# Gate and value projections of two transformer layers: seven block products in place of eight

## The chip, the cores and the metric

The kernel runs on one core of a Trainium2 chip. The metric is the device time of one execution in microseconds (us), lower is better; the number that counts is the median over runs. All data are float32.

The core has a matrix engine (TensorE, "PE" in the profile; its weight loads are the row "PEld"), a vector engine (VectorE, "DVE"), an activation engine (ScalarE, "ACT"), GpSimd ("POOL") and SyncE ("SP"), which here only issue DMAs. They run in parallel and meet through semaphores. TensorE writes to eight PSUM banks of 128 x 512 float32.

## The reference

The first block has two layers over 256 tokens of width 1024. Each layer is

```
ada = silu(c) @ w_ada[l] + b_ada[l]            # six sections: sh1, sc1, g1, sh2, sc2, g2
u = h * (1 + sc1) + sh1
y = mixer(u, w_in, ...)                        # mLSTM + dilated attention, then
                                               # (sig(g_a)*(a @ w_a) + sig(g_b)*(b @ w_b)) @ w_out
h = layer_norm(ALPHA * h + g1 * y) * ln1_g + ln1_b
u = h * (1 + sc2) + sh2
y = (silu(u @ w1) * (u @ w3)) @ w2             # w1, w3: 1024 x 2816; w2: 2816 x 1024
h = layer_norm(ALPHA * h + g2 * y) * ln2_g + ln2_b
```

The second block (256 latent and 256 context tokens) is a windowed attention with an MLP ("attn"), then a gated linear attention with an MLP ("gla"; 256 tokens only). It takes its modulation `ada` from its own matrix for two conditions.

## The kernel before

**Panels.** All weights come from HBM in half panels of 4 k-tiles x 512 columns (1 MB), through a ring of `RING` = 7 slots in SBUF. SyncE (L2951) loads half panel n once half panel n-7 has been released; TensorE releases a panel by an increment that rides on one of its next matmuls (`release`, L528).

**PE's order** is written out by hand in `@block.tensor` (L482). `feature_tiles` (L541) computes two feature tiles (128 features each) for all 256 tokens: 16 matmuls of 128 x 128 weights on 256 moving columns. One such call is one PSUM bank. The profile shows two records for each float32 matmul: 32 for such a call.

**PSUM banks** are handed out by `open_tile` (L485): a new tile takes the next of the eight banks in turn, and TensorE first waits until the tile that held this bank eight openings ago is drained:

```
b = st["next"]
...
if b in st["tenant"]:
    drained(*st["tenant"][b])
```

**End of the mixer (L817 to L828).** The products with `w_a` and `w_b` ("WA 0" to "WA 3", "WB 0" to "WB 3", two feature tiles each) are mixed on VectorE into `MIX` (L2410 to L2427). TensorE waits for "mix 3" and then runs the output projection "WO" (four tiles of 8 matmuls on 512 columns). VectorE adds the residual and normalises token tile 0, then token tile 1 (L2429 to L2433).

**Gate and value projections (L828 to L846).** TensorE transposes token tile 0 (`tile_transposes("U", 0)`), and ScalarE modulates it into `UT`. `half_tiles` (L572) then computes W1 0 and W3 0 for token tile 0 alone; it waits for the first half of the modulated features ahead of k = 0 and for the second ahead of k = 4. Token tile 1 is transposed and modulated (first half by ScalarE, second by VectorE, L2434), the second half of W1 0 and W3 0 follows, and then `feature_tiles` for W1 j, W3 j, j = 1 to 10. ScalarE takes silu of each W1 tile; VectorE multiplies with W3 (L2437 to L2442). A product of a W1 and a W3 panel has 8 blocks: k halves (2) x feature halves (2) x token halves (2).

**VectorE beside that (L2436 to L2454).** `affine("U")` (L1998): four operations of 128 x 1024 on the residual. Then the modulation turns: `ada_turn` (L2294) multiplies one 1 MB piece of `w_ada` (two operations of 128 x 1028 for one condition, four for two) and frees its slot; GpSimd (L2962) loads the next piece into one of two slots. Layer 0 takes 12 such turns here, layer 1 takes 20, of which 16 have two conditions. Engines work in order: whatever stands behind a waiting operation waits too.

**Winograd's form of Strassen's product** is in the kernel already, for W2 (L857 to L889, with `down_sums`) and for the MLPs of the second block (`fast_mlp`, L965, L2612): seven block products in place of eight, with sums of weight quarters (`panel_sums`, L2546), sums of token blocks (`token_sums`, L2565) and sums of the products (`first_sum`, L2582, and `product_sums`, L2589) on VectorE. `ORDER` is (1, 2, 4, 5, 7, 6, 3). The first panel goes by `FIRST_ORDER` (1, 2, 5, 7, 6, 3, 4): products 1 and 2 need token tile 0 alone. In the MLP of gla, a block product is 8 matmuls on 128 moving columns: the shape that the change uses.

Of the kernel before, what the change touches and what calls it, by code (L numbers as in the profile page):

```python
# [23 lines left out]
P = 128  # L24
# [223 lines left out]
def program(nc, a, out, marks):  # L248
    with ExitStack() as ctx:
# [183 lines left out]
        def combos(stage, nh):  # L433
# [5 lines left out]
                    for l in range(2) for w in ("w_mlp_in", "w_mlp_out", "w2")}  # L439
# [9 lines left out]
        down_out = area(M2["UT2"], KD, 2 * T)  # L449

# [31 lines left out]
        def _(pe):  # L482
# [151 lines left out]
            for l in range(DEPTH):  # L634
# [203 lines left out]
                j = 2  # L838
                for p in range(1, 6):
                    w1, w3 = panel(), None  # L840
                    for n in range(2 if p < 5 else 1):
                        feature_tiles(f"W1 {j}", w1, n, UT)
                        w3 = w3 or panel()
                        feature_tiles(f"W3 {j}", w3, n, UT)
                        j += 1
                    release(w1 + w3)  # L846
# [486 lines left out]
        def _(act):  # L1333
# [86 lines left out]
            for l in range(DEPTH):  # L1420
# [136 lines left out]
                act.wait_ge(dve_done, DV.at("h U"))  # L1557
                layer_params(l + 1)

                act.wait_ge(dve_done, DV.at("ln1 1"))  # L1560
                act.dma_start(ctx_early, a["ctx"].rearrange("(t p) n -> p t n", p=P)).then_inc(params_in, 16)
                if l == DEPTH - 1:
                    act.dma_start(area(M["CST"] + 2 * P, NC2), a["consts_attn"]).then_inc(par2_in, 16)
                for j in range(FFT // 2):
                    if j >= 4:
                        act.wait_ge(dve_done, DV.at(f"W3 {j - 4} drained"))
                    act.wait_ge(pe_done, PE.at(f"W1 {j} full"))
                    drain(f"W1 {j}", sg[:, j % 4, :], ACT.Silu).then_inc(act_done, AC.drained(f"W1 {j}"))
# [372 lines left out]
        def _(dve):  # L1941
# [143 lines left out]

            def down_sums(p, kg, i):
# [213 lines left out]
            for l in range(DEPTH):  # L2300
# [87 lines left out]
                for u in range(SLOTS // 2):  # L2388
# [14 lines left out]
                    for n in (2 * u, 2 * u + 1):  # L2403
                        dve.wait_ge(act_done, AC.at(f"slot exp {n}"))
                        V.reciprocal(att[:, n % 2, 3, :], att[:, n % 2, 2, :]).then_inc(dve_done, DV.step())
                        dve.wait_ge(dve_done, DV.count)
                        for tt in range(NT):
                            ts(SC[n % 2][:, tt, :], SC[n % 2][:, tt, :], att[:, n % 2, 3, tt:tt + 1], None, ALU.mult).then_inc(
                                dve_done, DV.step(f"probs {n}" if tt else None))
                for p in range(2):  # L2410
                    for n in range(2):
# [5 lines left out]
                            dve_done, DV.drained(f"WA {j}"))  # L2417
                    for n in range(2):
# [16 lines left out]
                dve.wait_ge(rows2_in, 16 * (l + 1))  # L2435
                affine("U")  # L2436
                for j in range(FFT // 2):  # L2437
                    dve.wait_ge(pe_done, PE.at(f"W3 {j} full"))
                    ps = tile(f"W3 {j}")
                    dve.wait_ge(act_done, AC.at(f"W1 {j} drained"))  # L2440
                    tt_(GT[:, 2 * j:2 * j + 2, :].rearrange("p a b -> p (a b)"), ps[:, :], sg[:, j % 4, :], ALU.mult).then_inc(
                        dve_done, DV.drained(f"W3 {j}"))  # L2442
                    if j < 2:
                        for q in turns[2 * j:2 * j + 2]:
                            ada_turn(q, [("ada", 0)])
                        if j == 1:
                            gate("g2")
                    elif j < 6:
                        for q in range(2 * j - 4, 2 * j - 2):
                            ada_turn(q, [("next", 0)] if l + 1 < DEPTH else [("next", 1), ("nextx", 2)])  # L2450
                    elif j < 10 and l == DEPTH - 1:
                        for q in range(2 * j - 4, 2 * j - 2):
                            ada_turn(q, [("ada", 1), ("adax", 2)])
                    if j == 8:  # L2454
                        down_token_sums(0, 0)
                down_sums(0, 0, 5)
# [88 lines left out]

            def panel_sums(name, n, i, after):  # L2546

                a11, a12, a21, a22 = quarters(n)
                if i == 5:
                    for m in (n, n + 1):  # L2550
                        dve.wait_ge(panel_in[m % RING], 16 * (m // RING + 1))
                    if after:
                        dve.wait_ge(pe_done, PE.at(f"{after} full"))
# [490 lines left out]
```

## Time and profile before

| | us |
|---|---|
| median of 3 runs | 2424.16 (2416.7 to 2425.68) |
| profiled execution | 2416.46, its span 2414.7 |
| TensorE busy | 2324.4 (96%) |
| VectorE busy | 1253.5 (52%) |
| ScalarE busy | 494.2 (20%) |
| gate and value stage, layer 0 (446 to 600) | TensorE 154.00 of 154, VectorE 47.22, DMA share 0.65 |
| gate and value stage, layer 1 (1097 to 1252) | TensorE 153.86 of 155, VectorE 108.43, DMA share 0.79 |
| mean granted TensorE clock | 0.992 of full |

A timeline row tells: start and duration in us, engine, line, operation, output <- input with shapes, count, and in brackets the idle time of that engine ahead of it with what ended it. Rows that stand close are merged ("x56"). "PEclk" is the granted clock, 1.00 for 2.4 GHz and 0.50 for 1.2 GHz.

### The profile page before, as it was taken

How to read it: one execution, taken by the hardware profiler on the slowest of the kernel's cores; microseconds unless marked ns; L12 is line 12 of the kernel's file. 1: busy time of each engine (PE TensorE's matmuls, PEld its weight loads, DVE VectorE, ACT ScalarE, POOL GpSimd, SP SyncE). 2: the span in 40 equal slices, each digit the busy share in tenths (PEclk: the TensorE clock that was granted, in tenths of full speed). 3: DMA queues.
4: the chain of work that ended last, by engine and by line, in shares of the span. 5: the costliest groups of instructions: out<-in, count | busy, mean ns of one | idle time of the engine just before them, and what ended most of it. 6: DMA issues, size and time to landing. Idle time of an engine off the chain costs nothing.

```text
span 2414.7 us, 27153 instructions
## 1 busy us (share of the span) xinstructions
PE 2324.4 (96%) x10982; PEld 1835.2 (76%) x10982; DVE 1253.5 (52%) x2360; ACT 494.2 (20%) x1048; POOL 62.6 (3%) x93
## 2 busy tenths in 40 slices
PE   7999999999999999999999999999999999888998
PEld 5888587788768876868887655588888874567987
DVE  5764311432746432125777266775566455556666
ACT  1222320100011223101011355312200032432200
POOL 0100000000000000000000000000000000000000
PEclk9999999999999999999999999999999999999999
DMA  9853433674475333336874101433333245134442
GB/s 392 321 210 106 156 122 126 233 289 166 175 283 196 134 110 145 124 136 249 305 288 166 35 36 36 148 113 134 121 123 140 79 141 187 74 113 170 161 158 79
DMA packets 163499, 391.18 MB, mean 162 GB/s; under 512 B 6448, under 2 KB 10928, under 8 KB 160560
## 3 DMA queue, kind: packets, MB, share of 16 engines
q1 hardware_dynamic: 136736, 285.03, 32.7%
q0 software_dynamic: 24080, 93.69, 10.6%
q10 hardware_dynamic: 2560, 10.72, 1.2%
q8 instruction: 88, 1.44, 0.2%
q14 instruction: 35, 0.29, 0.0%
HBM read 388.37 MB, written 1.05 MB: 161 GB/s over the span
## 4 chain that ended last, share of the span: by engine, by line
PE 91%; DVE 4%; ACT 2%; DMA 1%; issue 1%; DVEq 0%; SPq 0%; ACTq 0%
PE bank L503 89%; DVE arena L1946 2%; PE bank L501 2%; ACT arena L1335 2%; DVE arena L1952 1%; DMA arena<-in_w_ada 1%; ACT arena L1338 1%; DVE arena L1949 0%; DMA arena<-in_x 0%; DVE arena L2827 0%; ACT L1335 0%; DVE arena L2084 0%; DVE arena L2011 0%; DVE arena L2015 0%; DVE arena L2859 0%
## 5 line engine op out<-in xcount | busy, mean ns | idle before, releaser
L503 PE MATMUL bank<-arena 128*128 128x256 f32 (+6 forms) x10494 | 2267.1, 384 | 47.4 <-ACT arena L1335 15.2
L503 PEld LDWEIGHTS bank<-arena 128*128 128x128 f32 (+2 forms) x10494 | 1777.0, 189 | 524.7 <-issue 283.7
L1946 DVE TENSOR_TENSOR arena<-arena 128x1024 f32<-128x1024 f32 (+9 forms) x497 | 374.8, 767 | 231.0 <-PE bank L503 194.3
L1952 DVE SCALAR_TENSOR_TENSOR arena<-arena 128x1028 f32<-128x1028 f32 (+6 forms) x367 | 304.5, 845 | 101.6 <-DMA arena<-in_w_ada 66.7
L1335 ACT ACTIVATE arena<-arena 128x512 f32<-128x512 f32 (+5 forms) x386 | 196.7, 533 | 709.8 <-DVE arena L1946 357.5
L1946 DVE TENSOR_TENSOR arena<-bank,arena 128x512 f32<-128x512 f32 (+3 forms) x123 | 83.7, 690 | 471.4 <-PE bank L503 445.0
L1338 ACT ACTIVATE arena<-bank 128x512 f32<-128x512 f32 (+1 forms) x227 | 127.4, 596 | 707.8 <-PE bank L503 667.2
L1335 ACT ACTIVATE arena<-bank 128x256 f32<-128x256 f32 (+2 forms) x99 | 41.3, 438 | 400.3 <-PE bank L503 399.6
L1946 DVE TENSOR_TENSOR arena<-arena,bank 128x256 f32<-128x256 f32 (+2 forms) x172 | 85.4, 521 | 64.6 <-PE bank L503 59.8
L2970 POOL DMA_DIRECT2D arena<-in_w_ada x88 | 61.8, 702 | 2141.4 <-DVEq L1961 2135.4
L1952 DVE SCALAR_TENSOR_TENSOR arena<-bank,arena 128x254 f32<-128x254 f32 (+2 forms) x184 | 78.0, 468 | 51.4 <-PE bank L501 35.2
L501 PE MATMUL bank<-arena 128*128 128x128 f32 x488 | 65.9, 286 | 33.3 <-DVE arena L1949 17.6
L501 PEld LDWEIGHTS bank<-arena 128*128 128x128 f32 x488 | 58.8, 147 | 44.7 <-issue 21.3
L1949 DVE TENSOR_SCALAR arena<-arena 128x512 f32<-128x512 f32 (+8 forms) x278 | 80.3, 322 | 20.5 <-ACT arena L1335 12.7
L1952 DVE SCALAR_TENSOR_TENSOR junk<-arena 128x1028 bf16<-128x1028 f32 x64 | 78.6, 1229 | 6.3 <-DVE arena L1952 2.3
L1952 DVE SCALAR_TENSOR_TENSOR arena<-arena,bank 128x512 f32<-128x512 f32 (+1 forms) x40 | 24.8, 645 | 101.3 <-PE bank L503 97.1
L1949 DVE TENSOR_SCALAR arena<-bank,arena 128x256 f32<-128x256 f32 (+1 forms) x112 | 46.5, 468 | 59.3 <-PE bank L503 36.2
L1335 ACT ACTIVATE arena<-bank,arena 128x128 f32<-128x128 f32 (+2 forms) x138 | 57.6, 486 | 78.7 <-PE bank L501 31.2
L1335 ACT ACT_TABLE_LOAD x46 | 59.0, 1283 | 4.2 <-PE bank L503 2.2
L2221 DVE BATCH_NORM_STATS2 arena<-bank 128x6 f32<-128x256 f32 x16 | 6.1, 423 | 28.7 <-PE bank L503 28.7
L2399 DVE TENSOR_REDUCE arena<-arena 128x2 f32<-128x1024 f32 x16 | 19.5, 1220 | 0.5
L2745 DVE TENSOR_REDUCE arena<-arena 128x2 f32<-128x1024 f32 x16 | 19.3, 1209 | 0.0
(31 smaller groups left out, 132.0 us busy)
## 6 DMA issues: line engine op xcount, KB each, us to landing
arena<-in_w_ada POOLq DMA_DIRECT2D x88, 1028.0 KB, 6.1
arena<-in_w_in SPq DMA_DIRECT2D x84, 1024.0 KB, 7.1
arena<-in_w SPq DMA_DIRECT2D x56, 1024.0 KB, 7.3
arena<-in_w_mlp_in SPq DMA_DIRECT2D x32, 1024.0 KB, 6.4
arena<-in_w_mlp_out SPq DMA_DIRECT2D x32, 1024.0 KB, 6.5
arena<-in_w_gla SPq DMA_DIRECT2D x12, 1024.0 KB, 7.3
arena<-in_w_ada SPq DMA_DIRECT2D x16, 514.0 KB, 19.2
arena<-in_w_a SPq DMA_DIRECT2D x8, 1024.0 KB, 6.9
```

The source lines that it names most:

```text
L501: ins = nc.tensor.transpose(out, lhsT, rhs)
L503: ins = nc.tensor.matmul(out, lhsT, rhs, start=start, stop=stop)
L1335: return nc.scalar.activation(out, x, f, **kw)
L1338: return nc.scalar.activation(out, tile(key)[:, :out.free_size()], f)
L1946: return V.tensor_tensor(out, x, y, op)
L1949: return V.tensor_scalar(out, x, s1, s2, op0, op1) if op1 is not None else V.tensor_scalar(out, x, s1, None, op0)
L1952: return V.scalar_tensor_tensor(out=out, in0=x, scalar=s, in1=y, op0=op0, op1=op1, **kw)
L2221: V.bn_stats(stats[:, 6 * tt:6 * tt + 6], ps[:, tt * T:tt * T + T]).then_inc(dve_done, DV.step())
L2399: V.reduce_max(att[:, n % 2, 0, :], x[:, :, :], AX.X).then_inc(dve_done, DV.step())
L2745: V.reduce_max(st_[:, 0, 0:2], lat, AX.X).then_inc(dve_done, DV.step())
L2970: pool.dma_start(adaw[:, n % ADA_SLOTS], half_source(job, q)).then_inc(ada_in[n % ADA_SLOTS], 16)
```

## The change

1. W1 and W3 are computed panel by panel (five panels of 512 columns each, in the order W1 0, W3 0, W1 1, ...), each with seven block products of 2 x 4 matmuls on 128 moving columns; each block product opens a bank. The last 256 columns ("W1 10", "W3 10") stay as they were.
2. VectorE forms the weight sums, token sums and product sums; ScalarE copies product 1 of each panel and takes silu in four blocks of each W1 panel; VectorE multiplies once for each pair of panels.
3. `affine("U")` becomes four single steps behind panels 2 to 5.
4. The last four modulation turns of the layer and the eight of the next one go from the gate and value stage to the mix. In layer 1, the turns 8 to 11 for the second block stay in the stage (behind panels 2, 4, 6 and 8), and 12 to 15 go to the start of the second block's attention.
5. ScalarE issues the loads of the next layer's parameters behind panel pair 3.

```diff
 # TensorE
-                w1, w3, tiles = panel(), panel(), {}
-                half_tiles(("W1 0", "W3 0"), (w1, w3), 0, 0, tiles)
+                def up(name, p, order):
+                    q = quarters(first_of[l, "w1"] + 2 * UP.index((name, p)))
+                    ops = {1: (q[0], up_x[0]), 2: (q[1], up_x[2]), 4: (q[3], up_sums[4]), 5: (down_sum, up_sums[5]),
+                           7: (q[2], up_sums[7]), 6: (q[0], up_sums[6]), 3: (q[1], up_x[3])}
+                    for i in order:
+                        key = f"{name} {p} {i}"
+                        ps = open_tile(key)
+                        if i in (4, 5, 6, 7):
+                            pe.wait_ge(dve_done, DV.at(f"U x{i}"))
+                        if i in (5, 7, 6, 3):
+                            pe.wait_ge(dve_done, DV.at(f"{name} {p} w{i}"))
+                        for e in range(2):
+                            for k in range(KH):
+                                mm(ps[:, e * P:e * P + P], ops[i][0][:, k, e * P:e * P + P], ops[i][1][:, k, :], ...)
+                w1, w3 = panel(), panel()
+                drained("U 0 0")
+                drained("U 0 1")
+                for name in ("W1", "W3"):
+                    up(name, 0, FIRST_ORDER[:2])
                 pe.wait_ge(dve_done, DV.at("ln1 1"))
                 tile_transposes("U", 1)
-                half_tiles(("W1 0", "W3 0"), (w1, w3), 0, 1, tiles)
-                feature_tiles("W1 1", w1, 1, UT)
-                feature_tiles("W3 1", w3, 1, UT)
...
+                for name, w in (("W1", w1), ("W3", w3)):
+                    up(name, 0, FIRST_ORDER[2:])
+                    release(w)
+                for name, p in UP[2:]:
+                    w = panel()
+                    up(name, p, ORDER)
+                    release(w)
 # VectorE
+            def up_panel(at):
+                name, p = UP[at]
...
+                panel_sums(key, n, 6, f"{key} 1", down_sum)
+                panel_sums(key, n, 3, f"{key} 2", down_sum)
+                first_sum(key, c, read)
+                if at + 1 < len(UP):
+                    panel_sums("{} {}".format(*UP[at + 1]), n + 2, 5, f"{key} 5", down_sum)
+                for _ in product_sums(key, c, read):
+                    pass
+                if name == "W3":
+                    dve.wait_ge(act_done, AC.at(f"gated {p}"))
...
+                    tt_(x, x, up_out("W1", p), ALU.mult).then_inc(dve_done, DV.step(f"up {p}"))
 ...
                 for p in range(2):
                     for n in range(2):
                         ... # WA j: multiply
+                        beside_mix(1)
                     for n in range(2):
                         ... # WB j: multiply, add, mark "mix j"
+                        beside_mix({0: 1, 1: 5, 2: 1, 3: 1}[j])
...
                         if half:
                             normalise_tile("ln1", tt)
+                    if half == 0:
+                        panel_sums("W1 0", first_of[l, "w1"], 5, None, down_sum)
                 tile_modulated("U", 1, (1,))
-                affine("U")
-                for j in range(FFT // 2): ...
+                dve.wait_ge(act_done, AC.at("U 1 0 drained"))
+                token_sums("U", up_x, [up_sums[i] for i in (5, 6, 4)], False, up_sums[7])
+                for at in range(len(UP)):
+                    up_panel(at)
+                    if 2 <= at < 6:
+                        affine_step("U", at - 2)
+                    if l == DEPTH - 1 and at in (2, 4, 6, 8):
+                        ada_turn(7 + at // 2, [("ada", 1), ("adax", 2)])
+                    if at == 7:
+                        down_token_sums(0, 0)
...
 # start of the attention, ahead of the rotary embedding
+            for q in range(12, 16):
+                ada_turn(q, [("ada", 1), ("adax", 2)])
```

## Rows read from the trace of the kernel before

**Rows 1.** The page: busy time by engine (us, share, instructions); shares of the chain.

```profile
PE 2324.4 (96%) x10982; PEld 1835.2 (76%) x10982; DVE 1253.5 (52%) x2360; ACT 494.2 (20%) x1048; POOL 62.6 (3%) x93
...
PE 91%; DVE 4%; ACT 2%; DMA 1%; issue 1%; DVEq 0%; SPq 0%; ACTq 0%
```

**Rows 2.** Timeline, ScalarE: start, us, engine, line, op, out<-in, count, [idle, releaser].

```profile
459.55 0.60 ACT L1338 ACTIVATE arena<-bank 128x512 f32<-128x512 f32 x1 [6.22 <-PE bank L503]
...
584.41 0.60 ACT L1338 ACTIVATE arena<-bank 128x512 f32<-128x512 f32 x1 [13.27 <-PE bank L503]
...
1110.76 0.60 ACT L1338 ACTIVATE arena<-bank 128x512 f32<-128x512 f32 x1 [5.69 <-PE bank L503]
...
1237.69 0.60 ACT L1338 ACTIVATE arena<-bank 128x512 f32<-128x512 f32 x1 [13.27 <-PE bank L503]
```

**Rows 3.** Windows (stretch, its us, busy by engine, PEclk, DMA share, GB/s); timeline.

```profile
2218.01:2230.52 12.51, 12.51 (x114) 12.51 (x113) 9.88 (x15) 3.40 (x9) 0.71 (x1) 1.00 0.73 255
...
2228.82 0.37 ACT L1335 ACTIVATE arena<-bank 128x256 f32<-128x256 f32 x1
...
2241.32 0.37 ACT L1335 ACTIVATE arena<-bank 128x256 f32<-128x256 f32 x1
```

**Rows 4.** Timeline, layer 1, from the output projection to the gate and value products.

```profile
1084.16 1.04 PE L501 MATMUL bank<-arena 128*128 128x128 f32 x8
1086.51 1.13 PE L503 MATMUL bank<-arena 128*128 128x128 f32 x8 [1.31 <-ACT arena L1335]
1087.82 6.52 PE L503 MATMUL bank<-arena 128*128 128x128 f32 x56 [0.18 <-ACT arena L1335]
...
1095.25 1.37 DVE L1949 TENSOR_SCALAR arena<-bank,arena 128x128 f32<-128x128 f32 x4 [5.77 <-PE bank L501]
1096.37 53.86 PE L503 MATMUL bank<-arena 128*128 128x128 f32 x277 [1.16 <-ACT arena L1335]
```

**Rows 5.** Timeline, first panel of the second block's last MLP.

```profile
2201.19 1.37 DVE L1949 TENSOR_SCALAR arena<-bank,arena 128x128 f32<-128x128 f32 x4 [7.20 <-PE bank L503]
...
2203.61 41.62 PE L503 MATMUL bank<-arena 128*128 128x128 f32 x356 [2.46 <-DVE arena L1946]
...
2210.74 2.49 DVE L1946 TENSOR_TENSOR arena<-arena 128x1024 f32<-128x1024 f32 x2 [0.24 <-DVE arena L1952]
...
2214.51 1.61 DVE L1946 TENSOR_TENSOR arena<-arena,bank 128x256 f32<-128x256 f32 x4 [0.30 <-PE bank L503]
```

**Rows 6.** Timeline, layer 1, end of the mix.

```profile
1048.19 0.69 DVE L1946 TENSOR_TENSOR arena<-bank,arena 128x512 f32<-128x512 f32 x1 [6.24 <-PE bank L503]
...
1051.65 0.69 DVE L1946 TENSOR_TENSOR arena<-bank,arena 128x512 f32<-128x512 f32 x1 [2.77 <-PE bank L503]
...
1055.12 0.69 DVE L1946 TENSOR_TENSOR arena<-bank,arena 128x512 f32<-128x512 f32 x1 [2.05 <-PE bank L503]
...
1056.59 27.73 PE L503 MATMUL bank<-arena 128*128 128x512 f32 x64 [1.51 <-DVE arena L1946]
```

**Rows 7.** Timeline, a turn with two conditions; the page's issues: KB each, us to landing.

```profile
1132.66 1.23 DVE L1952 SCALAR_TENSOR_TENSOR junk<-arena 128x1028 bf16<-128x1028 f32 x1
...
1137.63 0.08 DVE L1952 DVE_READ_ACCUMULATOR arena<-arena 128x1 f32 x1
...
arena<-in_w_ada POOLq DMA_DIRECT2D x88, 1028.0 KB, 6.1
```

**Rows 8.** Timeline and windows, TensorE and its clock after two idle stretches.

```profile
664.98 8.60 PE L503 MATMUL bank<-arena 128*128 128x512 f32 x16 [3.06 <-issue]
...
665.00:667.00 2.00, 2.00 (x3) 0.97 (x4) 0.13 (x1) 1.28 (x4) 0.00 (x0) 0.50 1.00 422
...
1570.73 197.46 PE L503 MATMUL bank<-arena 128*128 128x256 f32 x928 [2.99 <-DVE arena L1946]
...
1570.73:1574.00 3.27, 3.27 (x15) 2.88 (x16) 3.24 (x3) 0.00 (x0) 0.00 (x0) 1.00 0.00 0
```

**Rows 9.** Timeline, start of the second block's attention, VectorE.

```profile
1357.46 0.69 DVE L1946 TENSOR_TENSOR arena<-bank,arena 128x512 f32<-128x512 f32 x1 [23.84 <-PE bank L503]
```

More of the change, by code:

```diff
@@ L829, in _ @@
                 tile_transposes("U", 0)
-                w1, w3, tiles = panel(), panel(), {}
-                half_tiles(("W1 0", "W3 0"), (w1, w3), 0, 0, tiles)
+                def up(name, p, order):
[11 more added lines that the diff above has]
+                            for k in range(KH):
+                                mm(ps[:, e * P:e * P + P], ops[i][0][:, k, e * P:e * P + P], ops[i][1][:, k, :], start=(k == 0),
+                                   stop=(k == KH - 1), done=key if e and k == KH - 1 else None)
@@ L847, in _ @@
+                for name, p in UP[2:]:
+                    w = panel()
+                    up(name, p, ORDER)
+                    release(w)
+                w1, w3 = panel(), panel()
+                feature_tiles("W1 10", w1, 0, UT)
+                feature_tiles("W3 10", w3, 0, UT)
+                release(w1 + w3)
                 gate_row("g2", adac[:, 5, :])
@@ L1555, in _, with first_up @@
                 tile_modulated("U", 1, (0,))
[L1557 to L1568, printed above, removed]
+                def first_up(name, p):
+                    if name == "W1" and p >= 2:
+                        act.wait_ge(dve_done, DV.at(f"up {p - 2}"))
+                    act.wait_ge(pe_done, PE.at(f"{name} {p} 1 full"))
+                    func(up_blocks(name, p)[1, 2], tile(f"{name} {p} 1")[:, :2 * P].rearrange("p (a b) -> p a b", a=2),
+                        ACT.Copy).then_inc(act_done, AC.drained(f"{name} {p} 1"))
@@ L1569, in _ @@
+                act.wait_ge(dve_done, DV.at("up 3"))
+                act.wait_ge(pe_done, PE.at("W1 10 full"))
+                drain("W1 10", sg[:, 2, :], ACT.Silu).then_inc(act_done, AC.drained("W1 10"))
                 gate_row("g2", 1)
@@ L2086, in down_sums, with affine_step @@
+            def affine_step(tag, n):
+                x = H[:, n % 2, :]
+                if n == 0:
+                    dve.wait_ge(rows2_in, 16 * (l + 1))
+                dve.wait_ge(dve_done, DV.count)
+                tt_(x, x, rows[:, n // 2, :], ALU.add if n >= 2 else ALU.mult).then_inc(
+                    dve_done, DV.step(f"h {tag}" if n == 3 else None))
             def down_sums(p, kg, i):
@@ L2409, in _, with beside_mix @@
                                 dve_done, DV.step(f"probs {n}" if tt else None))
+                beside = iter([(q, [("ada", 0)]) for q in ADA_TAIL] +
+                              [(q, [("next", 0)] if l + 1 < DEPTH else [("next", 1), ("nextx", 2)]) for q in ADA_NEXT])
+                def beside_mix(n):
+                    for _ in range(n):
+                        q, conds = next(beside)
+                        ada_turn(q, conds)
+                        if q == ADA_TAIL[-1]:
+                            gate("g2")
                 for p in range(2):
@@ L2433, in _ @@
                             normalise_tile("ln1", tt)
+                    if half == 0:
+                        panel_sums("W1 0", first_of[l, "w1"], 5, None, down_sum)
                 tile_modulated("U", 1, (1,))
-                dve.wait_ge(rows2_in, 16 * (l + 1))
-                affine("U")
[L2437 to L2454, printed above, removed]
+                dve.wait_ge(act_done, AC.at("U 1 0 drained"))
[6 more added lines that the diff above has]
+                        ada_turn(7 + at // 2, [("ada", 1), ("adax", 2)])
+                        if at == 8:
+                            gate("next g1")
+                            gate("next g1x")
+                    if at == 7:
                         down_token_sums(0, 0)
+                dve.wait_ge(pe_done, PE.at("W3 10 full"))
+                dve.wait_ge(act_done, AC.at("W1 10 drained"))
+                tt_(GT[:, 20:22, :].rearrange("p a b -> p (a b)"), tile("W3 10")[:, :], sg[:, 2, :], ALU.mult).then_inc(
+                    dve_done, DV.drained("W3 10"))
                 down_sums(0, 0, 5)
```

161 lines of the change are left out of this document (93 added, 68 removed).

## The prediction

> **What bounds the kernel now.** I read the page first: TensorE is busy 96% of the span and carries 91% of the chain of waits [rows 1]; VectorE is half idle. So fewer matmul columns are worth their full time, and VectorE work is free only as long as no matmul waits for it. Next the timeline of the stage: ScalarE drains W1 tile 1 at 459.55 and W1 tile 10 at 584.41 in layer 0, nine equal steps of 13.87 us, each a W1 and a W3 tile of 32 records [rows 2]. TensorE never stops there. In layer 1 the same nine steps take 126.93 us, 2.07 more [rows 2]: TensorE waits there some tenths at each panel pair, for weights, while more modulation loads share the DMA engines. The other ends of the argument are the few places where TensorE does wait: at the mix, at the two transposes ahead of the stage, and wherever eight banks are not enough.
>
> **Term 1, seven products for eight.** A 512-column panel of W1 or W3 costs 13.87 us now. The new panel has 7 x 8 matmuls on 128 columns, 112 records. The last MLP of the kernel runs just this shape, with the same sums on VectorE: its panels follow each other after 12.50 us (ScalarE's copy of product 1 at 2228.82 and 2241.32), with TensorE never idle and at full clock [rows 3]. That is 111.7 ns a record. Count from the restart of TensorE behind the second transposes, 1096.37 in layer 1 [rows 4]. Before: to the end of W3 10, that is to 1237.69 + 6.93 (one more tile, half of 13.87), 148.2 us; in layer 0 2.1 less, 146.2. After: what is left of the first pair is 10 products of 16 records, 17.9; then 8 panels, 100.0; then the unchanged W1 10 and W3 10, 13.9; together 131.8. Gain: 14.4 in layer 0, 16.4 in layer 1. I let the 2.1 of weight waits go with it: slots of the ring are now released panel by panel, and most turns have left the stage.
>
> A rule of the Trainium skill speaks against this. In rows 3 weight loads are busy for all of the 12.51 us too: at 128 columns they only just fit behind the matmuls. "TensorE: Matmul & The Clock Gate", section "Back-to-back issue gap", says that in a stream of load and matmul pairs both set the pace, about 81 ns for each at 128 columns against some 56 for the matmul alone. By that ratio (an estimate: 12.5 x 81/56) a panel would take 18.1 us and the change would lose 80 us. The trace disagrees: a record takes 111.7 ns, which is twice the page's lone matmul and leaves no room for more, and the trace decides.
>
> **Term 2, the first token tile.** Before, TensorE resumes behind the transposes (1084.16 + 1.04) at 1086.51, when half the features are modulated, does 8 records, and goes on at 1087.82 with 56 [rows 4]. After, it waits for both halves: start 1087.8, 64 records of 111.7 ns, 7.15 us, end 1094.95 instead of 1094.2. Cost 0.8, and an idle stretch of 2.6 in one piece.
>
> **Term 3, the second token tile.** Before, VectorE begins its half of the modulation at 1095.25 and TensorE needs only ScalarE's half to restart at 1096.37 [rows 4]. After, product 5 needs the first token sum, which stands behind VectorE's half. The same seam stands in the last MLP: VectorE starts at 2201.19, TensorE at 2203.61, 2.42 later [rows 5]. Shifted by 0.8, VectorE starts at 1096.05, TensorE at 1098.5. Terms 2 and 3 together: 2.1 later than 1096.37, idle 2.4.
>
> **Term 4, a bank that comes free late.** Products 1 and 2 of W1 0 and W3 0 are opened ahead of the second transposes. Counting openings: W3 0's product 2, two transposes, then W1 0's 5, 7, 6, 3, 4 - so W3 0's product 5 is the eighth behind W3 0's product 2 and gets its bank. That bank is drained by `first_sum` of W3 0, which VectorE reaches only in the second call of `up_panel`: behind the last sums of W1 0 (they wait for product 4, the last of `FIRST_ORDER`) and behind two weight sums of W3 0. From the end of product 4: four sums 1.61, two weight sums 2.49, one sum 0.42, by rows 5, and a few tenths to and from the semaphores: 4.9 us in which TensorE stands, once in each layer. The last MLP has one panel where this stage has two, so its trace doesn't show the wait. Bounds: 0 if I have miscounted the banks, 4.9 if not; I take 4.9. Further on I find none: product j of a panel takes the bank of product j-1 of the panel before, drained some products earlier.
>
> **Term 5, turns in front of "mix 3".** A turn with two conditions takes 5.05 us (1132.66 to 1137.71), one with a single condition half, 2.53; a load 6.1 us [rows 7]. VectorE now meets, in layer 1: WA 3 at 1048.19 (0.7, turn, to 1053.9), WB 2 (1.45, turn, to 1060.4 or so), WB 3 (1.45). "mix 3" comes at 1061.9, against 1056.55 before, when VectorE was on time for each tile [rows 6]. TensorE has nothing else: 5.4 us lost, 6.9 idle in one piece. In layer 0 the turns are half as long: VectorE is free for WB 3 half a microsecond late, cost 0.5. The five turns behind WB 1 lie under four tiles of gate products (WA 2 comes 33 us later): at two slots and 6.3 us a load they take 27. The twelfth turn and two weight sums fit into the 7 us that each WO tile takes (27.73 for four, [rows 6]) beside 2.1 of residual work.
>
> **What costs nothing, and its cover.** VectorE's sums: per panel 4 weight sums of 1.24 and 7 product sums of 0.42, 7.9 us, so 17.0 for a pair with its multiplication, against 25.0 of TensorE. In layer 1, pairs 1 and 2 also carry two affine steps (2.5) and a turn (5.1): 24.6. It fits by 0.4; if not, TensorE waits by the difference, some us in all. At its tightest (turn behind a W1 panel) the weight sum for product 6 is done 8.3 us into the next panel and wanted at 8.9. The four turns at the attention's start (20.2, with two loads to wait for about 22) stand where VectorE now idles 23.84 us until 1357.46 [rows 9]; the rotary result is wanted some 10 us later still. ScalarE's extra work and the later parameter loads have tens of us.
>
> **Sum on full clock.** Layer 0: -14.4 + 2.1 + 4.9 + 0.5 = -6.9. Layer 1: -16.4 + 2.1 + 4.9 + 5.4 = -4.0. Together -10.9.
>
> **Term 6, the clock.** The trace shows the granted clock at 0.50 (1.2 GHz) after some idle stretches: after 3.06 us idle, 16 records on 512 columns take 8.60 instead of 6.93 [rows 6, 8], 1.7 lost. After 2.99 us idle it stayed at 1.00 [rows 8]. Over the whole timeline I count nine stretches of 2.1 to 3.7 us: six were followed by a fall, three not; both of over 5 us were; none up to 1.8 was. The 2.46 in rows 5 was: from 2203.61 to the end of the panel's product 4 at about 2214.4 is 10.8 for 80 records, 8.9 at full pace. The change makes new idle stretches: 6.9 once, 4.9 twice, 2.4 to 2.6 four times, 2.0 once. Expected loss: three falls of 1.7, 5.1; four at two in three, 4.5; together 9.6 (0 to 13.6).
>
> Total: -10.9 + 9.6 = -1.3 us. Against the profiled execution's 2416.46 that gives 2415.2. The median of the runs shown, 2424.16, is 7.7 higher than that execution, and three runs already spread by 9; I apply the difference to the median: 2423.
>
> **Rivals.**
> A. *Clearly faster.* The bank is free in time, or VectorE reaches it earlier, and the clock stays up: -10.9 - 9.8 + 3 = -17.7, 2406. For it: term 1 is as sure as rows 3. Against: the counting in term 4, and rows 8. Chance 0.19.
> B. *The loads of the turns come late.* In the mix the turns are fed through two slots. Up to 8 us a load nothing more happens (the slot for WB 2's turn has 1.9 to spare over 6.1); at one and a half times the median, 9.2, the chain to "mix 3" ends 6 later in layer 1 and 2 later in layer 0: total +7, 2431; with a clock that falls at each new idle stretch, +11. For it: every turn's load now falls into 70 us beside panels. Against: the median load takes 6.1 [rows 7]. Chance 0.10.
> C. *Weight loads set the pace of the narrow matmuls.* In this stage's own 128-column records, 56 took 6.52, 116.4 ns each [rows 4], not 111.7. At that pace 20 panels lose 0.53 each, 10.6: total +9, 2433. From 112.3 ns a record on the change is slower than before, from 117.7 by over 12 us. For it: weight loads have no idle time in rows 3. Against: those 56 records carry the start behind a wait, and the 112 of rows 3 don't. The rule of the Trainium skill under term 1 would be this case at its worst. Chance 0.07.
> D. *The forecast*, within some us of no change: 0.64.
>
> **How the numbers follow.** About 0.5%, 12 us, is what a measurement can tell from no change. A lies beyond it mostly (0.17), and the forecast's own spread (clock losses 0 to 13.6, terms 2 to 5 each by 1) reaches it in a few cases: faster 0.20. B and C cross 12 us in their upper half, and the forecast's upper end adds a little: slower 0.13. Same: 0.67. Range: down to A and a lucky median, 2405; up to C with all clocks falling, 2436.
>
> **What would show it.** In the changed trace: ScalarE's product-1 copies 12.5 apart in both layers (term 1), TensorE idle about 4.9 ahead of the sixth product behind the second transposes (4), 6.9 ahead of WO in layer 1 and 2.0 in layer 0 (5), the seam's 2.4 (3), and granted clock 0.50 behind them (6). The forecast is wrong if W3 0's product 5 starts without a wait, if panels are not 12.5, or if VectorE is late in pairs 1 and 2 of layer 1.

## The result and the profile after

| | us |
|---|---|
| before, median of 20 runs beside it | 2422.16 (2416.63 to 2426.26) |
| after, median of 20 runs | 2426.31 (2419.88 to 2430.89) |
| ratio | 1.0017, 95% interval 1.0009 to 1.0024 |
| profiled execution after | 2429.7, its span 2427.8 |

The changed kernel is 4.15 us slower; the interval puts that between 2.2 and 5.8 us. It lies within 0.5%, and the interval excludes both no change and the forecast gain of 1.3 us. The stated range, 2405 to 2436, holds it, but that range is 31 us wide and tests little of the working.

The page of the kernel after: busy time by engine, the shares of the chain, and the group of the modulation turns' multiplications with the idle time ahead of it.

```profile
PE 2314.2 (95%) x11814; PEld 1854.0 (76%) x11814; DVE 1406.9 (58%) x2578; ACT 506.2 (21%) x1088; POOL 62.6 (3%) x93
...
PE 86%; DVE 6%; DMA 3%; ACT 3%; issue 2%; DVEq 0%; SPq 0%; ACTq 0%
...
L2002 DVE SCALAR_TENSOR_TENSOR arena<-arena 128x1028 f32<-128x1028 f32 (+6 forms) x367 | 304.5, 845 | 125.6 <-DMA arena<-in_w_ada 90.7
```

Beside [rows 1], TensorE has 10 us less work, VectorE 153 us more. What is new is the chain: its DMA share went from 1% to 3%, and TensorE's from 91% to 86%. Something that was hidden has come onto the path. The timeline of TensorE shows where; layer 0 first, then layer 1, from the output projection on (the bracket at the end of a row is the idle time ahead of it).

```profile
407.14 29.43 PE L518 MATMUL bank<-arena 128*128 128x512 f32 x64 [1.98 <-DVE arena L1996]
440.26 7.38 PE L518 MATMUL bank<-arena 128*128 128x128 f32 x64 [2.81 <-ACT arena L1368]
450.82 9.17 PE L518 MATMUL bank<-arena 128*128 128x128 f32 x80 [2.30 <-ACT arena L1368]
464.60 17.67 PE L518 MATMUL bank<-arena 128*128 128x128 f32 x135 [4.61 <-issue]
...
1068.95 30.08 PE L518 MATMUL bank<-arena 128*128 128x512 f32 x64 [11.57 <-DVE arena L1996]
1102.71 7.38 PE L518 MATMUL bank<-arena 128*128 128x128 f32 x64 [2.81 <-ACT arena L1368]
1113.27 10.80 PE L518 MATMUL bank<-arena 128*128 128x128 f32 x80 [2.30 <-ACT arena L1368]
1128.68 41.52 PE L518 MATMUL bank<-arena 128*128 128x128 f32 x356 [4.61 <-issue]
```

Eight idle stretches, of 1.98 to 11.57 us. Seven are the forecast's, to some tenths (2.0, 2.6, 2.4 and 4.9 in layer 0; 2.6, 2.4 and 4.9 in layer 1). The eighth, ahead of the output projection of layer 1, was to be 6.9 and is 11.57. Before, it was 1.51 [rows 6].

ScalarE's copies of product 1 of successive panels (timeline, layer 1):

```profile
1141.13 0.39 ACT L1368 ACTIVATE arena<-bank 128x256 f32<-128x256 f32 x1 [14.89 <-PE bank L518]
...
1153.63 0.38 ACT L1368 ACTIVATE arena<-bank 128x256 f32<-128x256 f32 x1 [0.60 <-PE bank L518]
...
1178.72 0.38 ACT L1368 ACTIVATE arena<-bank 128x256 f32<-128x256 f32 x1 [0.59 <-PE bank L518]
```

They are 12.50 apart, and 25.09 for the next two: the pace of [rows 3].

### The profile page after: what moved, and what is told of

It is laid out like the page before. It is cut to its first block, busy times and chain, and to the rows that moved or that the text cites. A ratio compares the mean times of both kernels' runs of the same rounds, so it can differ in the third digit from the quotient of the medians.

```text
span 2427.8 us, 29309 instructions
## 1 busy us (share of the span) xinstructions
PE 2314.2 (95%) x11814; PEld 1854.0 (76%) x11814; DVE 1406.9 (58%) x2578; ACT 506.2 (21%) x1088; POOL 62.6 (3%) x93
## 4 chain that ended last, share of the span: by engine, by line
PE 86%; DVE 6%; DMA 3%; ACT 3%; issue 2%; DVEq 0%; SPq 0%; ACTq 0%
PE bank L518 85%; DMA arena<-in_w_ada 3%; DVE arena L2002 2%; DVE arena L1996 2%; PE bank L516 2%; ACT arena L1368 2%; ACT arena L1371 1%; DVE junk L2002 1%; DVE arena L1999 1%; DMA arena<-in_x 0%; DVE arena L2919 0%; ACT L1368 0%; DVE arena L2134 0%; DVE arena L2061 0%; DVE arena L2065 0%
## 5 line engine op out<-in xcount | busy, mean ns | idle before, releaser
L518 PE MATMUL bank<-arena 128*128 128x256 f32 (+3 forms) x11326 | 2257.8, 368 | 71.3 <-DVE arena L1996 24.8
L518 PEld LDWEIGHTS bank<-arena 128*128 128x128 f32 (+1 forms) x11326 | 1796.6, 191 | 519.7 <-issue 296.6
L1996 DVE TENSOR_TENSOR arena<-arena 128x1024 f32<-128x1024 f32 (+7 forms) x595 | 489.5, 835 | 258.6 <-PE bank L518 217.6
L1368 ACT ACTIVATE arena<-arena 128x512 f32<-128x512 f32 (+5 forms) x426 | 213.5, 522 | 828.7 <-DVE arena L1996 456.4
L1371 ACT ACTIVATE arena<-bank 128x512 f32<-128x512 f32 (+1 forms) x207 | 115.3, 595 | 490.2 <-PE bank L518 450.4
L1996 DVE TENSOR_TENSOR arena<-bank,arena 128x512 f32<-128x512 f32 (+3 forms) x103 | 69.8, 690 | 226.7 <-PE bank L518 207.2
L1996 DVE TENSOR_TENSOR arena<-arena,bank 128x256 f32<-128x256 f32 (+2 forms) x312 | 140.6, 475 | 97.4 <-PE bank L518 88.6
L1368 ACT ACTIVATE arena<-bank 128x256 f32<-128x256 f32 (+2 forms) x119 | 48.8, 430 | 509.3 <-PE bank L518 484.1
```

Source lines behind the costliest of these rows:

```text
L518: ins = nc.tensor.matmul(out, lhsT, rhs, start=start, stop=stop)
L1368: return nc.scalar.activation(out, x, f, **kw)
L1371: return nc.scalar.activation(out, tile(key)[:, :out.free_size()], f)
L1996: return V.tensor_tensor(out, x, y, op)
```

## Where the 11.57 us come from

The chain of waits of the kernel after, from the first turns in the mix to the output projection (start, duration, what was waited for or ran):

```profile
1009.49 8.63 DMA arena<-in_w_ada
1018.15 1.25 DVE junk L2002 x2
...
1023.56 8.70 DMA arena<-in_w_ada
1032.28 1.25 DVE junk L2002 x2
...
1037.69 9.64 DMA arena<-in_w_ada
1047.35 1.25 DVE junk L2002 x2
...
1052.76 9.42 DMA arena<-in_w_ada
1062.21 1.25 DVE junk L2002 x2
...
1067.48 0.70 DVE arena L1996
1068.20 0.70 DVE arena L1996
...
1068.95 6.47 PE bank L518 x9
```

Four times in a row the chain goes through a load of modulation weights, and each takes 8.6 to 9.6 us where the prediction counted 6.1 to 6.3. The two slots do not hide that. A turn of two conditions takes 5.05 us (5.3 with what lies between two), and the slot it frees is wanted again after one more turn. With a load of 8.7, a pair of turns takes 8.7 + 5.3 = 14.0 us: the turns at 1018.15 and 1032.28 are 14.1 apart, not 10.5. The five turns behind WB 1 still end before WA 2 comes, but the slots then hand their lateness on: VectorE waits 3.11 us for the load of the turn behind WA 2 (at 1047.35 in its timeline) and 2.11 for that behind WB 2 (at 1062.21), 5.2 together. VectorE finishes "mix 3" at 1068.90; TensorE's last product for it ended at about 1057.4 (1068.95 less the 11.57 of its wait).

Why the loads are slow, by windows of the same trace (stretch, its us, busy time of PE, PEld, DVE, ACT, POOL, PEclk, share of the DMA engines' time, GB/s). The first two are loads of layer 0's mix, 364.28 to 370.13 and 372.87 to 382.99; the others are loads of layer 1's.

```profile
364.30:370.10 5.80, 5.80 (x28) 5.08 (x27) 2.39 (x4) 0.00 (x0) 1.39 (x2) 1.00 0.74 270
372.90:383.00 10.10, 10.10 (x48) 8.81 (x48) 2.40 (x5) 0.60 (x1) 1.37 (x2) 1.00 1.04 402
1009.50:1018.10 8.60, 8.60 (x41) 7.50 (x41) 3.62 (x6) 0.60 (x1) 1.40 (x2) 1.00 1.03 390
1037.70:1047.30 9.60, 9.60 (x46) 8.37 (x45) 5.49 (x9) 0.88 (x1) 1.40 (x2) 1.00 0.92 356
1052.80:1062.20 9.40, 4.58 (x22) 3.66 (x20) 6.84 (x11) 0.00 (x0) 1.37 (x2) 0.89 1.02 380
```

At 0.74 of the DMA engines' time the load takes 5.8 us, and SyncE's queue moves 0.31 MB of panels beside it. In the other windows that queue moves 1.07 to 2.10 MB, the share is 0.92 to 1.04, and a load takes 8.6 to 10.1. The Trainium skill, "DMA: Bandwidth & Descriptors", section "Issuing engines are not separate DMA queues", says that DMAs of different engines run on the same 16 DMA engines and interleave. These rows agree: GpSimd's own queue gives the turns no bandwidth of their own.

So the loads were late in layer 0 too, but there a turn has one condition, 2.5 us of work, and the gate products hid it. VectorE's timeline, the turn that waited longest for its load, and WA 2:

```profile
382.99 1.23 DVE L2002 SCALAR_TENSOR_TENSOR arena<-arena 128x1028 f32<-128x1028 f32 x1 [6.46 <-DMA arena<-in_w_ada]
...
391.33 0.69 DVE L1996 TENSOR_TENSOR arena<-bank,arena 128x512 f32<-128x512 f32 x1 [5.96 <-PE bank L518]
```

After 6.46 us of waiting for a load VectorE is still 5.96 us early for WA 2.

## The clock behind the new idle stretches

Windows of the kernel after, from the end of five of the eight idle stretches, in order of time.

```profile
407.00:411.00 4.00, 3.86 (x6) 1.83 (x7) 1.82 (x4) 0.00 (x0) 0.00 (x0) 0.64 1.03 399
464.60:468.60 4.00, 4.00 (x19) 4.00 (x20) 0.11 (x1) 0.00 (x0) 0.00 (x0) 0.50 0.86 284
...
1068.90:1073.00 4.10, 4.05 (x5) 1.85 (x6) 3.90 (x7) 0.00 (x0) 0.00 (x0) 0.50 0.96 285
1113.30:1117.00 3.70, 3.70 (x23) 3.70 (x24) 3.56 (x5) 0.62 (x1) 0.00 (x0) 0.68 0.00 0
1128.70:1132.70 4.00, 4.00 (x23) 4.00 (x24) 0.41 (x1) 0.00 (x0) 0.00 (x0) 0.62 1.02 413
```

The granted clock fell at these five; the blocks behind the other three, of 2.81, 2.30 and 2.81, run at full pace (7.38, 9.17 and 7.38 us). Against the full pace, 27.73 for the four tiles of the output projection and 111.7 ns for a 128-column record, and against the 9.17 that the same 80 records take in layer 0, the blocks are 1.7, 2.6, 2.4, 1.6 and 1.8 us too long: 10.1 together, where 9.6 was forecast.

## The experiments

Ratios are against the kernel before, run beside each batch. "Wait" is TensorE's idle time in the profile.

| kernel | median us | ratio, 95% interval |
|---|---|---|
| the change | 2426.31 | 1.0017, 1.0009 to 1.0024 |
| bank: first sum earlier | 2411.95 | 0.9957, 0.9943 to 0.9971 |
| half loads in layer 1's mix | 2423.73 | 1.0003, 0.9994 to 1.0012 |
| two turns moved, layer 1 | 2417.59 | 0.9984, 0.9975 to 0.9994 |
| before, with the moved turns only | 2433.45 | 1.0046, 1.0031 to 1.0061 |
| bank and turns | 2405.59 | 0.9928, 0.9912 to 0.9944 |
| split wait | 2423.52 | 1.0011, 1.0001 to 1.0020 |
| seam | 2423.5 | 1.0014, 1.0005 to 1.0023 |
| all of them | 2394.45 | 0.9891, 0.9876 to 0.9906 |
| bank, all turns in the stage | 2438.22 | 1.0079, 1.0057 to 1.0102 |

**The bank.** Is the idle stretch ahead of W3 0's product 5 the late first sum of W3 0?

```diff
-                first_sum(key, c, read)
+                if at != 1:
+                    first_sum(key, c, read)
+                if at == 0:
+                    first_sum("W3 0", up_blocks("W3", 0), ...)
```

> The changed kernel, but VectorE takes the first product sum of W3 0 (it drains the bank of product 2) in the call of W1 0, ahead of the weight sums. Theory (term 4: the eighth opening behind meets a bank that VectorE drains too late): the wait of 4.61 us ahead of W3 0's product 5 goes in both layers, and with it the fall of the clock behind it (up to 1.7 each): 9.2 to 12.6 us less than the changed kernel, ratio to the kernel before 0.9965 to 0.998. Rival (the wait is for the weight sums of W3 0, the bank only comes beside): the wait stays above 3 us and the time within 2 us of the changed kernel.

Timeline of TensorE in this kernel, the restart behind the second transposes, both layers:

```profile
448.64 33.62 PE L518 MATMUL bank<-arena 128*128 128x128 f32 x299 [2.31 <-ACT arena L1368]
...
1101.60 78.58 PE L518 MATMUL bank<-arena 128*128 128x128 f32 x686 [2.31 <-ACT arena L1368]
```

No wait is left where 4.61 stood in each layer. By the ratios this is 14.5 us below the change: 9.2 of waits, 4.4 of slow clock behind them (2.6 and 1.8 above), and 0.5 of the wait ahead of layer 1's output projection, 11.04 here, make 14.1. That is more than the 9.2 to 12.6 that were expected: the two falls of the clock cost 4.4, not up to 3.4, and the change of 0.5 at the output projection was not in it. Term 4 and its mechanism are shown. Term 1 is shown too, in the time itself: the kernel with the moved turns alone (below) lacks only the products and what belongs to them, and stands 0.0089 higher, 21.6 us, give or take 5 by the two intervals. By the terms: 30.8 of products, less 1.6 of weight waits that leave with the turns, 4.2 for terms 2 and 3 and 1.7 for a fall of the clock at 1101.60, 23.3.

**Half loads.** This kernel loads only half of each of the 12 pieces that layer 1's mix uses; VectorE's operations are the same, on partly stale values.

```diff
-                pool.dma_start(adaw[:, n % ADA_SLOTS], half_source(job, q))...
+                c = slice(0, 1) if 24 + 12 <= n < 24 + 24 else slice(0, 2)
+                pool.dma_start(adaw[:, n % ADA_SLOTS, c], half_source(job, q)[:, c])...
```

> The changed kernel, but the twelve pieces of w_ada that layer 1's mix uses are loaded only by half (512 KB each; the other half of a slot keeps what was there, so those modulation values are not the reference's). VectorE does the same operations. Theory (the loads are late in the mix of layer 1: 8.6 to 9.7 us each beside the panels, not the 6.1 of term 5): TensorE's wait ahead of WO falls from 11.57 to the 6.9 of the prediction, time 4 to 6 us less than the changed kernel, ratio about 1.000. Rival (the turns' own length and order cost it all): the wait stays at 11 us or more.

TensorE's timeline at the output projection of layer 1:

```profile
1061.56 30.48 PE L518 MATMUL bank<-arena 128*128 128x512 f32 x64 [7.43 <-DVE arena L1996]
```

TensorE's wait ahead of the output projection falls from 11.57 to 7.43. With loads in time the forecast had said 6.9, so VectorE's work in front of "mix 3" was counted right, and the other 4.1 us are the loads. The time follows less than that: 0.0014 lower, 3.4 us where 4 to 6 were expected, and the two intervals overlap a little. With loads in time the other half of the slot rule shows as well: three turns in a row free their slots at 1017.33, 1022.60 and 1027.87 (GpSimd's timeline), 5.27 apart, so VectorE's work alone sets the pace there.

**Two turns moved.** In layer 1 the turns behind WA 3 and WB 2 go behind the first residual and panel W3 0.

```diff
-                        beside_mix(1)
+                        beside_mix(0 if l and j == 3 else 1)
-                        beside_mix({0: 1, 1: 5, 2: 1, 3: 1}[j])
+                        beside_mix({0: 1, 1: 5, 2: 0 if l else 1, 3: 1}[j])
+                        if (half, tt) == (0, 0) and l:
+                            beside_mix(1)
+                    if at == 1 and l:
+                        beside_mix(1)
```

> The changed kernel, but in layer 1 the turns behind WA 3 and WB 2 are taken later: one behind the first WO tile's residual, one behind panel W3 0. Theory (term 5 with late loads): TensorE's wait ahead of WO in layer 1 falls from 11.57 to 1.5 to 4 us, and less of the half clock behind it: 8 to 12 us less than the changed kernel, ratio 0.9965 to 0.9985. Rival (the two turns do the same harm where they stand now, ahead of the normalisation and in the first panels): the wait ahead of WO goes, but the stage starts or runs later by as much, ratio above 1.000.

TensorE's timeline in layer 1, at the output projection and at the two new waits in the panels:

```profile
1056.15 27.73 PE L518 MATMUL bank<-arena 128*128 128x512 f32 x64 [1.51 <-DVE arena L1996]
...
1134.96 12.74 PE L518 MATMUL bank<-arena 128*128 128x128 f32 x112 [0.79 <-DVE arena L1996]
1149.49 30.73 PE L518 MATMUL bank<-arena 128*128 128x128 f32 x273 [1.79 <-DVE arena L1996]
```

The wait is back at 1.51, the block behind it at full clock, and two new waits of 2.6 stand where the moved turn meets the first panel pair. Behind the first transposes the clock fell in this execution (64 records in 9.01 us in place of 7.38), and behind the second it did not, which evens out. Net 7.5 less idle and 2.4 less of slow clock make 9.9; the ratios give 0.0033, 8.0 us.

**The moved turns alone**, with the eight products and the affine of before:

```diff
+                        beside_mix(1)                                # behind WA j
+                        beside_mix({0: 1, 1: 5, 2: 1, 3: 1}[j])      # behind WB j
-                    if j < 2: ...                                    # the turns in the stage
+                    if 6 <= j < 10 and l == DEPTH - 1:
```

> The kernel before, with its eight block products, but with the twelve turns of each layer at the mix, as the change puts them. Theory: this part alone costs the waits ahead of WO (0.5 in layer 0, 10 in layer 1) and 2 to 4 us of half clock, and gives back the 2.1 of weight waits in layer 1: 9 to 13 us more than before, ratio 1.004 to 1.0055; the block products by themselves are then worth 5 to 9 us. Rival (the block products are what loses): ratio below 1.002.

TensorE's timeline at the output projection of layer 1:

```profile
1069.31 30.02 PE L503 MATMUL bank<-arena 128*128 128x512 f32 x64 [10.84 <-DVE arena L1946]
```

0.0046 slower, 11.1 us: 9.3 of new idle in layer 1, 0.5 in layer 0 and 2.3 of slow clock make 12.1. So the products and what belongs to them bring 0.0029, 7.0 us, inside the change. By the terms and the rows it should be 30.8, less 1.6 of weight waits, 4.2 for terms 2 and 3, 9.2 for term 4, 6.0 of slow clock behind the restarts and 0.7 of a longer wait at the output projection: 9.1. The interval of this kernel's ratio, 3.6 us either way, holds it. ScalarE's drains of W1 1 and W1 10 in layer 1 (1125.74 and 1251.05 in its timeline) are 125.3 us apart, not 126.93 [rows 2]: 1.6 of the 2.1 us of weight waits went with the turns, as term 1 assumed.

**Bank and turns together**, with the affine steps two by two behind panels 2 and 4 and layer 1's turns behind panels 1, 3, 5, 8 and 9, so that no panel has both.

> The changed kernel with both mends: the early product sum of W3 0 and, in layer 1, the two turns behind WA 3 and WB 2 taken behind the first WO tile and behind panel W3 0. The order of VectorE's extras in layer 1's stage is changed too (turns behind panels 1, 3, 5, 8, 9, affine steps in pairs behind 2 and 4), since a turn behind panel 1 with the old order made TensorE wait 0.79 and 1.79 us. Theory: the two mends add up: 14.4 and 8.7 us of their own, 21 to 25 less than the changed kernel, 2402 to 2406, ratio 0.991 to 0.993. Rival (VectorE, with less slack in layer 1, becomes the limit of the stage once the bank wait is gone): waits for the weight sums of 1 to 5 us at several panels, ratio above 0.994.

TensorE's timeline in layer 1, the output projection and the one wait left in the panels:

```profile
1052.51 27.73 PE L518 MATMUL bank<-arena 128*128 128x512 f32 x64 [1.51 <-DVE arena L1996]
...
1125.29 54.88 PE L518 MATMUL bank<-arena 128*128 128x128 f32 x488 [0.78 <-DVE arena L1996]
```

0.9928. One stage wait of 0.78 is left of the 2.6, and the two edits add up: 0.0060 + 0.0033 would have made 0.9924.

**Split wait.** At token tile 0, product 1 of both panels needs only the first half of the modulated features.

```diff
-                drained("U 0 0")
-                drained("U 0 1")
-                for name in ("W1", "W3"):
-                    up(name, 0, FIRST_ORDER[:2])
+                for h in range(2):
+                    drained(f"U 0 {h}")
+                    for name in ("W1", "W3"):
+                        up(name, 0, FIRST_ORDER[h:h + 1])
```

> The changed kernel, but TensorE waits only for the first half of token tile 0's features ahead of product 1 of W1 0 and W3 0, and for the second half ahead of their products 2. Theory (term 2): the idle stretch behind the first transposes falls from 2.81 to about 1.5, the next work starts 1.3 earlier in each layer: 2.6 us less than the changed kernel, and up to 3 more where the clock fell behind it; ratio 0.9993 to 1.001. Rival (the normalisation of token tile 1 ends late anyway, so TensorE only waits there instead): no change of time.

TensorE's timeline in layer 1, the products of the first token tile:

```profile
1098.24 7.38 PE L518 MATMUL bank<-arena 128*128 128x128 f32 x64 [1.42 <-DVE arena L2134]
```

The wait is halved, from 2.81 to 1.42, in both layers. The ratio of 1.0011 lies inside the interval of the change; alone it can't be told from it, and the expected 2.6 us are neither shown nor refuted by the time.

**Seam.** At token tile 1, ScalarE and VectorE change halves, and the sum for product 5 comes first.

```diff
-                tile_modulated("U", 1, (1,))
-                token_sums("U", up_x, ...)
+                tile_modulated("U", 1, (0,))
+                tt_(up_sums[5], up_x[1], up_x[0], ALU.subtract)...
+                # then, behind ScalarE's half: sums 7, 6, 4
```

> The changed kernel, but at the second token tile VectorE modulates the first half of the features and ScalarE the second, and the first token sum, which reads the first half alone, follows at once. Theory (term 3: the sum stands behind VectorE's half): TensorE's wait behind the second transposes falls from 2.30 to about 1.8, 0.5 us a layer; 1 us less than the changed kernel, or up to 4 less if the clock no longer falls behind it; ratio 1.000 to 1.0015. Rival (ScalarE's half, 1.5 us, sets it as before): the wait stays at 2.3.

TensorE's timeline in layer 1, the restart behind the second transposes:

```profile
1110.27 9.17 PE L518 MATMUL bank<-arena 128*128 128x128 f32 x80 [1.87 <-ACT arena L1368]
1124.39 55.80 PE L518 MATMUL bank<-arena 128*128 128x128 f32 x475 [4.96 <-issue]
```

2.30 becomes 1.87, but behind it the bank wait of layer 1 grows from 4.61 to 4.96: whoever starts earlier waits longer for the same sum. Its ratio of 1.0014 can't be told from the change.

**All of them**, and layer 0's turn behind WB 2 moved like layer 1's:

> All mends together: the early product sum, layer 1's two turns moved and the new order of its extras, layer 0's turn behind WB 2 moved behind the first WO tile, the split wait for token tile 0 and the swapped halves at token tile 1. Theory: they add up: 21 to 25 from the first two, 2.6 and 1 from the waits at the token tiles, 0.5 in layer 0: 25 to 31 us less than the changed kernel, 2396 to 2402, ratio 0.989 to 0.992. Rival (idle stretches under 3 us cost nothing beyond themselves and are made up elsewhere): no better than the two mends alone.

TensorE's timeline in layer 1, from the output projection on:

```profile
1047.53 27.73 PE L518 MATMUL bank<-arena 128*128 128x512 f32 x64 [1.51 <-DVE arena L1996]
...
1077.55 7.38 PE L518 MATMUL bank<-arena 128*128 128x128 f32 x64 [1.42 <-DVE arena L2134]
...
1087.67 27.04 PE L518 MATMUL bank<-arena 128*128 128x128 f32 x240 [1.86 <-ACT arena L1368]
1115.49 64.71 PE L518 MATMUL bank<-arena 128*128 128x128 f32 x576 [0.78 <-DVE arena L1996]
```

2394.45 us, ratio 0.9891 (0.9876 to 0.9906): it beats both kernels, by 26.5 us the one before. Every stretch in these rows is under 1.9 us, and the blocks of 64 and 240 records run at full pace behind them. Beyond the kernel with bank and turns it gains 0.0037, 9.0 us, of which the waits are 4.1 (0.5, 2 x 1.4, 2 x 0.4). The rest is clock, as far as one execution of each can tell. In the kernel with bank and turns, layer 0's output projection takes 29.43 and layer 1's 64 records of the first token tile 8.73, 1.7 and 1.3 over the full pace, and behind the seam's wait the clock fell in both layers, 1.6 each; here it fell at none of these places. The split wait, the seam and layer 0's turn were not tried one by one without the bank wait, so how much each brings here is not shown.

**All turns in the stage.** Was it necessary to move the turns at all? The bank kernel with no turn in the mix; layer 0 has one behind panels 1 to 7, two and three behind 8 and 9, layer 1 two behind panels 1 to 6, one or two behind 7 to 9.

> The first sum of panel W3 0 in the call of panel W1 0, as in the bank experiment, and all turns of the two layers left in the stage of the gate and value projections, none in the mix, as many behind each panel as the cores of VectorE's work allow (layer 0: one behind panels 1 to 7, two behind 8, three behind 9; layer 1: two behind panels 1 to 6, one or two behind 7 to 9). Theory: in layer 1 VectorE then has about 164 us of work (79 us of sums, 14 us for the rest of the stage, 70.7 us of turns) against some 125 us of TensorE's products, so TensorE waits for banks of PSUM; the time is some 20 us above the bank experiment (2412), so 2424 to 2440, ratio 1.001 to 1.008. Rival: VectorE's idle time around the stage covers the turns and only the wait ahead of WO goes, 11 back to 1.5 us: 2403, ratio 0.992. The wait ahead of WO 0 0 of layer 1 should be under 2 us by both.

The wait ahead of the output projection is back at 1.51 in both layers, and layer 0 shows none in the stage. Layer 1 does (TensorE's timeline, five of its eight waits in the panels):

```profile
1131.98 12.74 PE L518 MATMUL bank<-arena 128*128 128x128 f32 x112 [1.48 <-DVE arena L1996]
1153.05 14.47 PE L518 MATMUL bank<-arena 128*128 128x128 f32 x112 [8.33 <-DVE arena L1996]
1172.80 14.82 PE L518 MATMUL bank<-arena 128*128 128x128 f32 x112 [5.28 <-DVE arena L1996]
1193.88 14.53 PE L518 MATMUL bank<-arena 128*128 128x128 f32 x112 [6.26 <-DVE arena L1996]
1212.35 15.49 PE L518 MATMUL bank<-arena 128*128 128x128 f32 x112 [3.94 <-DVE arena L1996]
```

Panel by panel TensorE waits for VectorE, 28.4 us over the stage, and the four panels behind the waits of 3.94 and more are 1.7 to 2.8 longer by the clock; the one behind 1.48 isn't. The ratio lies where the expectation had it. Against the bank kernel: 0.0122, 29.5 us slower. So layer 1's stage can't hold all the turns beside the sums: the turns, or some of them, have to leave it. The two that were moved from in front of "mix 3" found a cheaper place.

## Why the prediction was wrong, step by step

**Failed: term 5's time for a load.** It took the median of all modulation loads, 6.1 us [rows 7], for loads that would stand beside panel loads at full rate. Against the warning of rival B, that "every turn's load now falls into 70 us beside panels", that median could say nothing: none of the 88 loads behind it runs in a mix. The chain after has 8.6 to 9.6 us four times, the wait became 11.57 in place of 6.9, and halving the loads took 4.1 of those 4.7 us back. That is rival B's mechanism, which had a chance of 0.10; it put the price at 8 us in both layers together, and the wait shows 4.7, all in layer 1. In layer 0 the wait came at 1.98 as forecast although loads were late there too, up to 10.1 us: rival B's 2 us for that layer were hidden under the gate products.

With that term at its measured size the sum at full clock is -10.9 + 4.7 = -6.2, and with 10.1 for the clock it is +3.9. Measured: +4.15.

**Right in sum, by luck in part: term 6.** The clock cost 10.1 against 9.6, but not where it was expected. The three stretches of 4.6 and more cost 6.8, not 5.1; of the four of 2.3 to 2.8 one was followed by a fall, not two or three, and cost 1.6, not 4.5; the one of 2.0, put at nothing, cost 1.7. The errors cancel. In other executions the same places behave otherwise: with half loads the 1.98 us in layer 0 cost nothing.

**Right:** term 1 (12.50 us a panel in both layers, no loss to weight loads, so rival C is out: 25.09 us for two panels is 112.0 ns a record); term 2 (2.81 against 2.6); term 3 (2.30 against 2.4); term 4 (4.61 against 4.9, in both layers, and gone with the first sum moved, so rival A is out); layer 0 of term 5 (1.98 against 2.0). The turns at the attention's start stayed hidden: they now fill VectorE's 23.84 us of idle time [rows 9], and TensorE's restart there, 1335.53, comes behind a wait of 2.20.

The Trainium skill's 81 ns for each load and matmul pair ("TensorE: Matmul & The Clock Gate", section "Back-to-back issue gap") would have made a panel 18.1 us, by the prediction's estimate. The copies 12.50 us apart in this trace disagree, as [rows 3] did.

**The rest of the two traces.** The spans of the two profiled executions differ by 13.1, not by 4. By TensorE's timelines, the stretches that the change touches make 4.0 of that: the waits ahead of the output projections are 0.5 and 10.1 longer, and from there to the end of each layer's MLP it takes 3.0 and 3.6 less (252.50 in place of 255.47, and 266.58 in place of 270.16). The other 9.1 lie in blocks with the same records in both: 1.3 ahead of layer 0's output projection, 3.5 between the two layers' (the longest such block takes 140.98 before and 144.31 after), 4.3 in the second block. They are one execution each: before's lay 5.7 under the median of its 20 runs, after's 3.4 above. The spread of one kernel's runs goes with its mean granted clock: of the 20 after, the three at 0.986 took 2419.9 to 2420.6, the one at 0.981 took 2430.9. The block of 140.98 and 144.31 took 140.98, 142.66 or 144.31 in the nine experiments too, 142.66 with the moved turns alone and 140.98 with all turns in the stage. Whether the change makes a fall of the clock there more likely is not shown.

## What to carry to other kernels

A wait that is forecast from a load's time needs the time of a load *in the stretch where it will stand*: read the DMA share there first, and where it is near 1 take the loads of such stretches, not the page's median. With two slots, work of T and a load of L, a pair of turns takes the larger of 2T and T + L (10.5 us with half loads, 14.1 in the change); from L = T on, each microsecond of load is one of delay. Then ask what hides that delay: here the gate products did in layer 0 and not in layer 1.

When seven products replace eight, list which bank the first panel's openings reuse and what drains it: here one 0.42 us sum in the wrong call cost 14 us, more than the rest of the change brought. And short idle stretches are best counted with the clock behind them: removing 4.61 us of wait twice gave 14.5, and in this kernel stretches under 1.9 us cost no clock in the rows shown. A trace is one execution: compare the stretches that the change touches, not the two spans.

## What the runs showed of the hardware

- A 1 MB load takes 5.8 us at a DMA share of 0.74, and 8.6 to 10.1 at 0.92 to 1.04, on a queue of its own.
- A fall of the clock after an idle stretch is no function of its length alone: at 2.30 us it fell in layer 1 and not in layer 0 in the same execution; at 1.98 it fell in the execution after (29.43 for the block) and not in the one with half loads (27.73 behind the same 1.98). Of the eight executions with this 1.98 us wait in layer 0, two have the fall: the change, and bank and turns.
